# Second expert weights loaded as two neighbouring rows per partition, and the transpose of the activations that goes with it

## What is computed

```python
def expert_rows(args):
    xe, e = args
    hh = xe @ w1[e] + b1[e]
    glu = jnp.minimum(hh[:, :D_FF], SWIGLU_LIMIT)
    lin = jnp.clip(hh[:, D_FF:], -SWIGLU_LIMIT, SWIGLU_LIMIT)
    act = glu * jax.nn.sigmoid(SWIGLU_ALPHA * glu) * (lin + 1.0)
    return act @ w2[e] + b2[e]
```

## Time and profile before

| | us |
|---|---|
| median of 3 runs | 1553.04 |
| lowest and highest of them | 1552.08, 1553.85 |
| the profiled execution | 1552.45 |
| its span, first to last instruction | 1550.7 |
| TensorE busy | 1478.0 (95%) |
| VectorE busy | 1329.0 (86%) |
| ScalarE busy | 1117.4 (72%) |
| HBM bytes moved by DMA, mean | 291 GB/s |

### The profile page before, as it was taken

How to read it: one execution, slowest core, us unless ns; L and a number is a source line. 1 busy time by engine, 2 the same in 40 slices (tenths; PEclk the granted TensorE clock), 3 DMA queues, 4 the chain that set the end, 5 groups by cost and what they waited for, 6 DMA issues and landing times.

```text
span 1550.7 us, 22355 instructions
## 1 busy us (share of the span) xinstructions
PE 1478.0 (95%) x7046; PEld 1192.4 (77%) x7046; DVE 1329.0 (86%) x1532; ACT 1117.4 (72%) x1313; POOL 232.8 (15%) x200
## 2 busy tenths in 40 slices
PE   6999998888999999999999999999999999999993
PEld 5788786776778888888888887888888888888872
DVE  5476655477999999999999999999999999999983
ACT  4466554354788888888888888888888888888873
POOL 5000000034011111111111111111111111111110
PEclk9999999988999999999999999999999999999997
DMA  7021121169899999999999999999999999999943
GB/s 235 25 82 41 42 82 55 43 265 362 325 372 360 374 357 360 370 369 365 367 368 364 358 357 368 357 367 365 352 363 371 365 370 362 368 356 367 353 152 124
DMA packets 100214, 451.88 MB, mean 291 GB/s; under 512 B 13504, under 2 KB 25792, under 8 KB 67408
## 3 DMA queue, kind: packets, MB, share of 16 engines
q1 hardware_dynamic: 90704, 434.55, 74.3%
q0 software_dynamic: 9472, 16.85, 4.4%
HBM read 445.05 MB, written 23.07 MB: 302 GB/s over the span
## 4 chain that ended last, share of the span: by engine, by line
PE 91%; DVE 4%; ACT 2%; DMA 1%; issue 1%; POOL 1%; POOLq 0%; SPq 0%; ACTq 0%; DVEq 0%
PE zpair L1885 45%; PE bank L1885 23%; PE bank L1545 4%; PE bank L1546 3%; PE bank L1547 3%; PE bank L1854 2%; PE bank L1860 2%; PE zpair L1617 1%; PE zpair L1869 1%; PE bank L1681 1%; PE bank L1632 1%; PE bank L1878 1%; DVE stage_lo L1079 1%; PE zpair L1605 1%; PE zpair L1653 1%
## 5 line engine op out<-in xcount | busy, mean ns | idle before, releaser
L723 ACT CAST stage_hi<-ring 128x1024 fp32r<-128x1024 f32 x796 | 835.5, 1055 | 222.3 <-PE zpair L1885 150.5
L1079 DVE TENSOR_TENSOR stage_lo<-ring,stage_hi 128x1024 fp32r<-128x1024 f32 x796 | 952.9, 1223 | 48.0 <-ACT stage_hi L723 13.7
L1885 PE MATMUL zpair<-stage_hi,act_hi 128*128 128x512 f32 x1024 | 324.1, 398 | 7.3 <-DVE stage_lo L1079 5.3
L1885 PE MATMUL zpair<-stage_hi,act_lo 128*128 128x512 f32 x1024 | 316.8, 391 | 0.0
L1885 PE MATMUL zpair<-stage_lo,act_hi 128*128 128x512 f32 x1024 | 316.7, 391 | 0.0
L1885 PEld LDWEIGHTS zpair<-stage_hi,act_hi 128*128 128x128 f32 x1024 | 188.0, 189 | 56.0 <-DVE stage_lo L1079 13.6
L1885 PEld LDWEIGHTS zpair<-stage_lo,act_hi 128*128 128x128 f32 x1024 | 193.0, 188 | 41.1
L1885 PEld LDWEIGHTS zpair<-stage_hi,act_lo 128*128 128x128 f32 x1024 | 192.8, 188 | 40.7
L1885 PE MATMUL bank<-stage_hi,act_hi 128*128 128x512 f32 x512 | 162.7, 399 | 0.1
L1885 PE MATMUL bank<-stage_lo,act_hi 128*128 128x512 f32 x512 | 159.4, 393 | 0.0
L1885 PE MATMUL bank<-stage_hi,act_lo 128*128 128x512 f32 x512 | 158.7, 391 | 0.0
(11 more groups left out here) (284 smaller groups left out, 1492.6 us busy)
## 6 DMA issues: line engine op xcount, KB each, us to landing
ring<-in_w SPq DMA_DIRECT2D x384, 1024.0 KB, 7.6
ring<-in_w_in SPq DMA_DIRECT2D x12, 1024.0 KB, 5.4
ring<-in_w_out SPq DMA_DIRECT2D x4, 1024.0 KB, 5.0
xs_all<-in_x SPq DMA_DIRECT2D x4, 512.0 KB, 7.5
ring<-in_x SPq DMA_DIRECT2D x4, 512.0 KB, 3.7
tn_scratch<-qk SPq DMA_DIRECT2D x4, 512.0 KB, 2.7
x_scratch<-ring SPq DMA_DIRECT2D x4, 512.0 KB, 3.8
ring<-x_scratch SPq DMA_DIRECT2D x4, 512.0 KB, 5.2
```

Of the source, the lines that this page charges most:

```text
L723: nc.scalar.copy(dst, src).then_inc(split_hi, 1)
L1079: nc.vector.tensor_tensor(dst, src, hi_ap.bitcast(F32), ALU.subtract).then_inc(split_lo, 1)
L1885: mm = pe.matmul(bank[b0 + h][:], w[:, k, :], m[:, j % STAGES, h * BANK:(h + 1) * BANK], start=False, stop=stop and w is T_lo)
```

## The change

A partition takes two neighbouring rows of `w2`. In the view of `w2` the 1024 rows are now 4 pieces x 128 partitions x 2 rows, so partition p of piece c gets rows 256c + 2p and 256c + 2p + 1. These lie one after the other in HBM, and the load is one run of 8 KB per partition. The first half slot of piece c then holds the even rows of its 256, and the second one the odd rows. To contract the right columns with them, the transpose with number k takes every second column of the 256 that begin at 256 (k // 2), from the even or the odd one on: its stationary operand is read with a step of two elements. Its result is again 128 x 128. All else (the number and order of the instructions on each engine, the waits, the bytes) stays.

```diff
-    w2_d = w2[0].rearrange("e (k p) n -> e k p n", p=P)
+    w2_d = w2[0].rearrange("e (c p i) n -> e c p (i n)", p=P, i=2)
...
                 else:
-                    k = 2 * (c - KT)
-                    src = w2_d[e_w2, k:k + 2].rearrange("k p n -> p k n") if isinstance(e_w2, int) else \
-                        w2_d[bass.ds(e_w2, 1), k:k + 2].rearrange("e k p n -> p (e k) n")
-                    sp.dma_start(slot(z).rearrange("p (k n) -> p k n", k=2), src).then_inc(full[z], 16)
+                    src = w2_d[e_w2, c - KT] if isinstance(e_w2, int) else \
+                        w2_d[bass.ds(e_w2, 1), c - KT].rearrange("e p n -> p (e n)")
+                    sp.dma_start(slot(z), src).then_inc(full[z], 16)
...
                 z = moe_slot(12 * E - 4 + c - KT)
-                k = 2 * (c - KT)
-                sp.dma_start(slot(z).rearrange("p (k n) -> p k n", k=2),
-                             w2_d[E - 1, k:k + 2].rearrange("k p n -> p k n")).then_inc(full[z], 16)
+                sp.dma_start(slot(z), w2_d[E - 1, c - KT]).then_inc(full[z], 16)
...
             def turn_a(t):
                 pe.wait_ge(act_made, t + 1)
                 for k in range(KT):
-                    mm = pe.transpose(bank[6 + k // 4][:, k % 4 * P:(k % 4 + 1) * P], lin[:, k * P:(k + 1) * P], identF[:])
+                    mm = pe.transpose(bank[6 + k // 4][:, k % 4 * P:(k % 4 + 1) * P], lin[:, k // 2 * 2 * P + k % 2:(k // 2 + 1) * 2 * P:2], identF[:])
                 mm.then_inc(a_turned, 1)
```

More of the change, by code:

```diff
@@ L541, in _ @@
                     z = moe_slot((24 * OVER - 8) // 2 + c - KT)
-                    k = 2 * (c - KT)
                     sp.wait_ge(*REST.freed(OVER - 1, c - KT))
-                    sp.dma_start(slot(z).rearrange("p (k n) -> p k n", k=2),
-                                 w2_d[bass.ds(el, 1), k:k + 2].rearrange("e k p n -> p (e k) n")).then_inc(full[z], 16)
+                    sp.dma_start(slot(z), w2_d[bass.ds(el, 1), c - KT].rearrange("e p n -> p (e n)")).then_inc(full[z], 16)
             sp.wait_ge(all_scattered, 1)
```

## The result

The changed kernel takes 1557.03 us in the median of 16 runs, the kernel before 1553.55 in its 16 beside them. The ratio is 1.0022 with a 95% interval of 1.0012 to 1.0032: slower by about 3.4 us (1.9 to 5.0). Forecast was no change. The whole interval lies above 1, so the loss is small but real.

A forecast was written before the change was run, and what follows sets the result against it. TensorE was taken as the bound; 1552.45 us profiled + 0 (loads) + 0 to 1.3 (transposes) gave 1552.45 to 1553.75, or 1553.0 to 1554.3 from the median. Forecast 1553.0 us, own range 1551 to 1556, wide range 1550.5 to 1566.

The forecast's parts named there:

- What bounds the kernel: Main loop: TensorE is the bound, busy 95% of the span, its pieces filling 36.02 of an item's 36.04 us.
- The loads, at 0: Loads of `w2`: 128 loads as 8 KB runs may land slightly earlier or later, costing and giving nothing.
- The margin: Loads into slots: about 32 us available, landing at most 19.0 us after issue, so at least 13 us spare.
- the row of `w1`: Loads of `w1`, 8 KB runs: median landing 8.2 us against 7.0, so `w2` might land 1.2 us later.
- Rival (c): Loads of `w2`: runs still cut into 4 KB packets, or landing as before; time as forecast, chance within the 0.79.
- Rival (b): Loads of `w2`: fewer, longer packets speed up SBUF's readers, at most 10.5 us faster (1542.5); chance 0.05.
- The transposes, "0 to 1.3 us, and in the sum 0": 256 transposes of `turn_a`, stationary operand read with a step of two: 0 to 1.3 us more, counted as 0.
- my chosen bracket: One strided transpose: 109 ns as now, up to 114 ns if 1024 bytes pass at 9.0 bytes per ns.
- a slower load shows in full: Transposes in a row: the weight load holds each at 109 ns, so any added load time lengthens the chain fully.
- Rival (a): Transposes of `turn_a`: the read with a step is slow, kernel slower by 12.8 us or 27.9 us; chance 0.16.
- the wide one: Whole kernel: the wider range of times, 1550.5 to 1566 us, leaving out a full doubling of the transposes.
- The price of 12.8 us: 256 transposes: weight load going from 139 to 189 ns, 50 ns more each, giving 1565.8 us.

The follow-up runs named there:

- load-only: The changed kernel with its transposes set back to contiguous reads, so only the loads of 8 KB runs differ from the kernel before: 1553.39 us, ratio 0.9994.

## Why the prediction was wrong, point by point

**What bounds the kernel: right.** TensorE's pieces add up to the item before (36.02 of 36.03 us) and after (36.10 or 36.11 of 36.12), and the item grew by what these pieces grew.

**The loads, at 0: right.** The margin held: load-only has a ratio of 0.9994, and in the changed kernel the median landing moved by 0.1 us, not by the 1.2 that the row of `w1` stood for. That the issue would fall to 333 ns, and the packets to 83,830, came out to the digit. Rival (c) is out. Rival (b) too: with the new loads alone VectorE's subtraction takes 1218 ns in the median, as in the earlier trace rows, and the 48 matmuls with `w2` take 11.17 us, as in the earlier trace rows.

**The transposes, "0 to 1.3 us, and in the sum 0": the step that failed.** The place was the right one (weight loads in a row of transposes, with nothing to hide in), the size was not. 8 transposes take 0.945 us, 118 ns each, where the top of my chosen bracket was 114, and the 42 matmuls behind them take 0.03 us more, a place that I had not costed at all. With the 48 matmuls with `w2`, shorter by 0.01 to 0.02, it is 0.086 us an item x 32 = 2.7 us, where I took 0. The sentence "a slower load shows in full" was wrong as well: a load 70 ns longer moved the transposes apart by 9 ns. The bracket rested on the moving operand's rate, 9.0 bytes per ns, as if bytes passed over were what is paid. The runs with other steps show that they aren't: step eight passes over four times the bytes of step two, in 110 ns.

The Trainium skill's rule on lines of 16 bytes ("Advanced Engine Details and Errata", section "SBUF Cachelines": two accesses on a line absorb the latency) would have made step two free and steps four and eight dear. Here two costs 118 ns, four 119 and eight 110. The measurement decides: for the stationary operand of these transposes the rule holds at neither end.

**Rival (a), at 0.16, is what happened, at its very edge and with prices that were too high.** It was to begin at 121 ns for a transpose, 3.1 us in all. It was 118, and with the matmuls behind the total is 2.7 us by the trace, under that line, and 3.4 by the ratio, over it, with 3.1 well inside the interval. The signs that I had set for it, 8 transposes in 1.2 to 1.7 us and an item of 36.4 to 36.9, did not come (0.945 and 36.117); they left the stretch from 0.97 to 1.2 without a sign. The measured 1557.03 us is above the forecast's own range, 1551 to 1556, and inside the wide one only because rival (a) had stretched it. The price of 12.8 us was read from the 189 ns of another weight load against 139, as if the load's own length were added to the path. It isn't: the load became 70 ns longer (139 to 209), and the transposes moved apart by 9; with step eight it is 49 ns longer, and they moved by 1. The loads overlap each other (209 ns long and 120 apart) and the matmuls, and what counts is the distance from one to the next, 0.87 / 8 in the earlier trace rows, which I had read and then left for the duration.

**The chances.** With no row of before for a strided read, and every bound on the side of a loss, a term of 1.3 us at its "nearest row" needed only to be wrong by a factor of 2.4 to cross the line of 3.1 us. 0.79 for no change was too much for that.

## What to carry to other kernels

A layout that makes a DMA's runs longer is worth nothing where the loads follow the computation, while what it asks of the engine that bounds the kernel is paid: look first at who must read with a step. When a layout leaves a choice of step, measure the distance between the instructions with each; here eight neighbouring rows per partition cost nothing that could be told, and two cost 0.2%. Price a change of an overlapped instruction by the distance from one to the next on the chain, never by its own duration.

## What the hardware showed that I had not expected

- The cost of a step in the stationary operand of a float32 transpose isn't monotonic: 8 transposes take 0.87, 0.945, 0.91, 0.955, 1.06, 0.97 and 0.88 us with steps of 1, 2, 3, 4, 6, 7 and 8 elements.
- A weight load's duration and its cost come apart: 188 ns and 139 ns loads both go at 109 to 110 ns from one transpose to the next. Above 188 ns the distance follows the load: 120 ns within the row at 209, and 136 at 239.
- Eight loads with a step of two cost 0.086 us an item in a row, and 0.008 with a matmul of 512 columns ahead of each; 16 in two groups cost 0.148, less than twice one group, while the transposes of both groups take the same 0.95 us.
- A matmul behind a single transpose takes some 0.235 us instead of 0.227, which makes a spread group dearer than one in a row (36.100 against 36.031 us an item).
